# Eight of the 48 modulation bundles leave TensorE's delta-rule chain and are weighed and added on VectorE beside the feed-forward steps

## What is computed

```python
mod = silu_c @ ada_w[i] + ada_b[i]        # [1024] @ [1024, 6 * 1024], for layers i = 0, 1
```

```python
def first_block(x, ...):
    for l in range(DEPTH):                                        # DEPTH = 1
        h = rmsnorm(x, ln1[l])
        proj = h @ w_in[l]
        y_a = gated_deltanet(qkv_a, z_a, b_a, a_a, ...)           # chunked, a triangular solve inside
        y_b = dilated_attention(...)
        x = x + jnp.concatenate([y_a, y_b], axis=-1) @ w_out[l]
        h = rmsnorm(x, ln2[l])
        gate = causal_dwconv(h @ w_gate[l], ffn_conv[l])
        x = x + (jax.nn.silu(gate) * (h @ w_up[l])) @ w_down[l]
    return rmsnorm(x, ln_f)
```

## Time and profile before

| | |
|---|---|
| median of 3 runs | 1216.68 us (1215.64 to 1217.39) |
| the profiled execution's own time | 1214.66 us |
| its span in the profile | 1212.9 us |
| TensorE busy | 1107.1 us, 91% |
| VectorE busy | 593.5 us, 49% |
| ScalarE busy | 431.6 us, 36% |
| GpSimd busy | 94.3 us, 8% |
| read from HBM, written | 351.89 MB, 7.36 MB |

### The profile page before, as it was taken

The page is one execution under the profiler, slowest core; times in us unless marked ns, Lnnn a source line. Parts: engine busy times, 40 slices in busy tenths (PEclk is TensorE's granted clock), DMA queues, the critical chain, the costliest instruction groups (busy, mean ns, idle before and its releaser), DMA issues.

```text
span 1212.9 us, 17412 instructions
## 1 busy us (share of the span) xinstructions
PE 1107.1 (91%) x6792; PEld 741.0 (61%) x6792; DVE 593.5 (49%) x1175; ACT 431.6 (36%) x737; POOL 94.3 (8%) x189
## 2 busy tenths in 40 slices
PE   6998798889999999988999999887999999999986
PEld 6876454779999978855744343324887854343422
DVE  3588543566666656747522322226765532323223
ACT  6445322364444555536411120104545441011200
POOL 0201232320000000013000000002000000000000
PEclk9999999989999999998999999999999999999999
DMA  9956799797777745693679999997676479999996
GB/s 297 263 190 210 273 328 336 203 368 238 212 232 226 227 131 173 209 359 146 265 290 409 409 409 409 409 409 262 224 275 233 142 282 411 409 408 410 409 409 240
DMA packets 164175, 356.15 MB, mean 294 GB/s; under 512 B 10617, under 2 KB 79481, under 8 KB 163969
## 3 DMA queue, kind: packets, MB, share of 16 engines
q1 hardware_dynamic: 147056, 295.81, 67.7%
q0 software_dynamic: 17024, 59.26, 13.9%
q10 hardware_dynamic: 16, 0.02, 0.0%
HBM read 351.89 MB, written 7.36 MB: 296 GB/s over the span
## 4 chain that ended last, share of the span: by engine, by line
PE 67%; DMA 16%; DVE 10%; ACT 4%; issue 2%; POOL 0%; SPq 0%; DVEq 0%; ACTq 0%; POOLq 0%
PE bank L573 35%; PE bank L1134 12%; PE bank L1144 8%; DMA ering<-in_ada_w 4%; DMA ering<-in_moe_w_up 3%; DMA work<-in_moe_w_up 3%; DMA a_raw<-in_moe_w_up 3%; PE bank L1103 3%; DVE wlo L563 2%; PE bank L518 2%; DMA work<-in_ada_w 1%; ACT whi L557 1%; PE bank L741 1%; DMA wraw<-in_w_up 1%; PE bank L1845 1%
## 5 line engine op out<-in xcount | busy, mean ns | idle before, releaser
L563 DVE TENSOR_TENSOR wlo<-wraw,whi 128x1024 fp32r<-128x1024 f32 x150 | 179.3, 1220 | 62.5 <-ACT whi L557 60.3
L557 ACT ACTIVATE whi<-wraw 128x1024 fp32r<-128x1024 f32 x150 | 153.9, 1053 | 55.6 <-PE bank L573 47.1
L573 PE MATMUL bank<-a_hi,whi 128*128 128x256 f32 x512 | 146.7, 287 | 1.5 <-DVE a_lo L771 1.4
L573 PE MATMUL bank<-a_lo,whi 128*128 128x256 f32 x512 | 145.2, 284 | 0.0
L573 PE MATMUL bank<-a_hi,wlo 128*128 128x256 f32 x512 | 145.1, 283 | 0.0
L1134 PE MATMUL bank<-ering,work 128*64 128x512 f32 x576 | 129.6, 595 | 9.4 <-DMA ering<-in_moe_w_up 5.0
L1334 DVE TENSOR_TENSOR work<-work,bank 128x512 f32<-128x512 f32 x16 | 11.0, 687 | 203.7 <-PE bank L1134 203.7
L573 PE MATMUL bank<-whi,a_hi 128*128 128x512 f32 x256 | 102.7, 401 | 4.8 <-DVE a_lo L771 3.0
L1242 ACT ACTIVATE o_hi<-work 128x512 fp32r<-128x512 f32 x32 | 20.2, 630 | 236.7 <-DVE work L1302 236.3
L573 PEld LDWEIGHTS bank<-a_hi,whi 128*128 128x128 f32 x512 | 98.5, 192 | 8.1 <-issue 6.1
L573 PE MATMUL bank<-whi,a_lo 128*128 128x512 f32 x256 | 100.5, 392 | 0.0
(11 more groups left out here) (328 smaller groups left out, 1861.8 us busy)
## 6 DMA issues: line engine op xcount, KB each, us to landing
ering<-in_moe_w_up SPq DMA_DIRECT2D x36, 1024.0 KB, 18.2
ering<-in_moe_w_down SPq DMA_DIRECT2D x36, 1024.0 KB, 18.1
ering<-in_moe_w_gate SPq DMA_DIRECT2D x36, 1024.0 KB, 17.2
ering<-in_ada_w POOLq DMA_DIRECT2D x52, 512.0 KB, 5.7
wraw<-in_w_in SPq DMA_DIRECT2D x28, 512.0 KB, 7.3
work<-in_ada_w POOLq DMA_DIRECT2D x28, 512.0 KB, 8.1
wraw<-in_a_w_qkv SPq DMA_DIRECT2D x24, 512.0 KB, 4.8
work<-in_moe_w_down SPq DMA_DIRECT2D x12, 1024.0 KB, 18.7
```

The costliest lines, as they stand in the source:

```text
L557: nc.scalar.activation(w_hi(c), wraw[:, c % RING, :], ACT.Copy).then_inc(w_hi_done, 1)
L563: nc.vector.tensor_tensor(w_lo(u[0]), wraw[:, u[0] % RING, :], w_hi(u[0]).bitcast(F32), ALU.subtract).then_inc(w_lo_done, 1)
L573: mm = nc.tensor.matmul(out_ap, l, r, start=first and n == 0, stop=last and n == len(terms) - 1)
```

## The change

Bundles 24 to 31 (`ADA_ADDED`) are no longer issued on TensorE. The chain's remaining calls of `ada` are renumbered so that only bundles 8 to 23 stand in it: four ahead of the levels in place of eight, ten in levels 1 to 5 as before, two behind them in place of six. The eight bundles are loaded into three other places of SBUF (11, 12 and 13 of the experts' ring): three of them at the start of the feed-forward layer, the other five during it, one each time that `mul_f` shows a place free. After step 3 + 2j + h VectorE weighs half h of bundle j with one column of silu(c) and adds it to bundle 24's place (`add_bundle`), 16 instructions of 128x1024 elements. VectorE's hardware loop over steps 3 to 20 is written out for that. Behind TensorE's last step four products with a tile of ones sum the weighed rows over the partitions into bank 3, ahead of bundles 35 and 36. Bundles 38 to 40 are loaded behind the last added one. `grow_add(1)` moves from the end of the chain to the first modulated layer, behind `shift_dve`, and the wait on it from the output projection to the second group of qkv columns. `acol_copy(0)` moves from ahead of the levels to level 3, `acol_copy(1)` from level 5 to behind the last copy of the chain.

```diff
-ADA_BANK = [7, 7, 7, 7, 2, 7]
+ADA_BANK = [7, 7, 7, 3, 2, 7]
...
-ADA_BLOCK = 32
+ADA_BLOCK = 24
+
+
+ADA_ADDED = range(24, 32)
+ADA_STEP = 3
...
             if ada_turn(n) > 1:
-                pool.wait_ge(ada_used, max(m for m in range(n) if ada_ring(m) == ada_ring(n)) + 1)
+                m = max(m for m in range(n) if ada_ring(m) == ada_ring(n))
+                if m == ADA_ADDED[0]:
+                    pool.wait_ge(ada_used, ADA_SUM)
+                elif m in ADA_ADDED:
+
+                    pool.wait_ge(mul_f, ADA_STEP + 2 * (m - ADA_ADDED[0]) + 3)
+                else:
+                    pool.wait_ge(ada_used, ada_count(m))
...
-            for n in range(ADA_NORM, ADA_FFN + 1):
-                if ADA_PLACE[n] == 11:
-                    pool.wait_ge(w_used, U_FFN)
+            pool.wait_ge(w_used, U_FFN)
+            for n in (*ADA_ADDED[0:3], *range(ADA_NORM, ADA_NORM + 3)):
                 load_ada(pool, n)
...
+            added = 3
+            for s_ in range(1, FF_STEPS):
+                pool.wait_ge(mul_f, s_)
...
+                if added < len(ADA_ADDED) and s_ == ADA_STEP + 2 * (added - 2) + 3:
+                    load_ada(pool, ADA_ADDED[added])
+                    added += 1
+            for n in range(ADA_NORM + 3, ADA_FFN + 1):
+                load_ada(pool, n)
...
-                ada(10 + c)
+                ada(9 + c)
...
-            ada(12)
+            ada(10)
...
-            ada(14)
+            ada(11)
...
-            ada(16)
+            ada(12)
...
-                ada(15 + 2 * n)
+                ada(11 + 2 * n)
...
-                ada(16 + 2 * n)
+                ada(12 + 2 * n)
...
-            ada(27)
+            ada(23)
...
-            ada(28)
+            ada(24)
...
-            ada(29)
...
-            ada(30)
...
-            ada(31)
...
-            ada(32)
...
             step_pe(pe, FF_STEPS - 1, None, 0)
+            pe.wait_ge(mul_f, ADA_STEP + 2 * len(ADA_ADDED) + 1)
+            for q in range(4):
+                mm = nc.tensor.matmul(psum[ADA_BANK[3]][32 * q:32 * q + 32, :], con[:, C_ONES:C_ONES + 32],
+                                      ada_part(ADA_ADDED[0], q // 2)[:, (q % 2) * HALF:(q % 2 + 1) * HALF], start=True,
+                                      stop=True)
+            mm.then_inc(ada_used, 1)
             ada(ADA_LASTS)
...
             router_weights(psum[3], 0)
-            n = (FF_STEPS - 4) // 2
-            with dve.Fori(0, n) as i:
-                hidden_dve(dve, 3, i, 6, lambda j: split_lo(dve, (nxt[0] + j, i, 6)))
-                hidden_dve(dve, 4, i, 6, lambda j: split_lo(dve, (nxt[0] + 3 + j, i, 6)))
-            nxt[0] += 6 * n
-            for s_ in range(3 + 2 * n, FF_STEPS):
+            def add_bundle(j, h):
+
+                n = ADA_ADDED[j]
+                if h == 0:
+                    dve.wait_ge(ada_in[ada_ring(n)], 32 * ada_turn(n))
+                acc, c = ada_part(ADA_ADDED[0], h), silc[:, j, 0:1]
+                if j == 0:
+                    link(nc.vector.tensor_scalar(acc, acc, c, None, ALU.mult))
+                else:
+                    link(nc.vector.scalar_tensor_tensor(out=acc, in0=ada_part(n, h), scalar=c, in1=acc, op0=ALU.mult,
+                                                        op1=ALU.add))
+
+            for s_ in range(3, FF_STEPS):
                 ffn_step(s_)
+                if 0 <= s_ - ADA_STEP < 2 * len(ADA_ADDED):
+                    add_bundle((s_ - ADA_STEP) // 2, (s_ - ADA_STEP) % 2)
```

49 lines of the change are left out of this document (27 added, 22 removed).

## The result

| | before | with the change |
|---|---|---|
| median | 1217.39 us (9 runs, 1215.64 to 1223.72) | 1209.87 us (9 runs, 1203.58 to 1214.06) |
| ratio, with its 95% interval | | 0.9934 (0.9914 to 0.9955) |
| the profiled execution's own time | 1214.66 us | 1207.93 us |
| its span | 1212.9 us | 1206.1 us |
| TensorE busy | 1107.1 us | 1105.2 us |

The change makes the kernel 7.5 us faster (by the interval, 5.5 to 10.5 us), inside the range of the prediction (1201.5 to 1212.0), with 4.1 us more time than its number, 1205.8. Of these, 0.7 us lie in the kernel before, whose median over nine runs is 1217.39 where the prediction had 1216.68; the gain is 7.5 us where 10.9 were forecast.

What follows compares the result with a forecast made beforehand. The delta rule's chain was taken to be partly led by bundles and their loads in TensorE's fixed order. -8.2 - 3.7 + 1.0 = -10.9 us gave 1203.8 profiled, 1205.8 as median (2.0 above); range 1201.5 to 1212.0.

Steps and rivals of the forecast that it cites:

- Ahead of the levels: Up to the first level: without four bundles VectorE becomes the bound and the first level starts at 149.6, saving 8.2 us.
- the 8 us among its signs: Ahead of the levels: the first level was to come 8 us after L2412's end instead of 18.
- The rival that something else held the chain: Whole chain: the bundles' time is merely relabelled as waiting, so no change, 1216.7 us; chance 0.04.
- Behind the levels: First to last set of `heads`: without bundles the sets follow only data, 8.5 us instead of 12.2, saving 3.7 us.
- The clock among the sets: Sets of `heads`: TensorE was taken to run at the full clock; a granted clock under 1 would show the prediction wrong.
- The second rival: Sets of `heads`: TensorE falls to the lower clock, six sets and the transposes 6 us longer, 1211.8 us; chance 0.11.
- The levels: Levels between the transposes and `heads`: they keep two bundles each and cost the same, 7.7 us for the first.
- Rival 3: Levels: loads of bundles 12 and 13 land up to 1 us late and still lead, 2 us lost, 1207.8; chance 0.08.
- The feed-forward layer: Feed-forward steps: the 16 VectorE adds cost nothing, covered by 1.2 us idle and 2.9 us slack per step; DMA share 0.85.
- Rival 4: Feed-forward layer: VectorE waits in its order for a late bundle, holding the next step; 1226 us if all five late; chance 0.05.
- The end of the layer: Behind TensorE's last feed-forward step: four more products on the path add 1.0 us.
- The tail: Bundle 35 to the end of the span: the distance was to stay at 772.5 us.

Runs made afterwards that it cites:

- the kernel with eight bundles there: The change's sixteen chain bundles placed eight ahead of the levels, two in each of levels 1 to 4, none from level 5 on: 1215.56 us, 0.9985 of the kernel before.
- The four resident products: The change plus four sets of bundle-shaped products on data already in SBUF, results unused, behind sets 1, 3, 5 and 6 of `heads`: 1204.39 us in one run.
- the weights held back: The change with SP's loads of the feed-forward weights held until bundle 23 is used: 1210.01 us in one run.
- The later bundles: The change with one bundle in level 5, 21 and 22 in the last level, 23 ahead of the last set of `heads`: 1203.69 us, 0.9903 of the kernel before.
- the runs with three and four adds: The change with each of VectorE's 14 adds of bundles 25 to 31 issued three or four times: feed-forward steps of 9.40 and 10.71 us in place of 8.5.

## Why the prediction was right, and where it was off

**Ahead of the levels: right.** Forecast -8.2 us, measured -8.3, with the first level at 150.01 (149.6 foreseen), and 18.9 to 19.0 us in all profiles of this code. VectorE was the bound, as the sum had it: the first level came 9.9 us behind the end of the operation that the prediction calls L2412. Its sum gives 10.0; the 8 us among its signs don't fit that sum and are a slip. That TensorE's order, led by loads, was what held it, is shown by the kernel with eight bundles there: 28.0 us, with the waits for loads back. The rival that something else held the chain is out.

**Behind the levels: right, with some luck.** Forecast -3.7, measured -3.6, the gaps among the sets those that were counted. In three other profiles of this code it was 0.6 to 0.9 us less. The four resident products show that the loads were the larger part of it.

**The clock among the sets: right in one profile, not in others.** It was 1.00 in the change's first profile (8.6 us), but 0.92, 0.93 and 0.89 in three others with the same code up to there (9.2 to 9.5 us), and 0.70 with eight bundles ahead (11.4 us). The prediction named a clock under 1 there as a sign that it is wrong. The second rival thus comes true in part and in a smaller size, 0.6 to 2.8 us where it said 6; and in the three profiles the clock had fallen behind a wait for bundle 23's load, not for want of fillers among the sets. The Trainium skill, "TensorE: Matmul & The Clock Gate" (Part 1, on oscillation), describes kernels whose clock goes up and down because matmuls stand between waits for DMA; that is the case at 182.95 us, and in the kernel with eight bundles ahead (0.70 over 141 to 157 us). The rule would have been worth more at the levels than at the sets.

**The levels: the step that failed.** "The levels keep two bundles each and cost the same", a term of nothing in the sum. Measured, from the first level to the first set: 44.5 us against 42.1, so 2.4 us, and 42.5 to 44.0 in four other profiles of this code, on average 1.5 us more. One part is the first level, 8.4 us in all five profiles where 7.7 were taken over from before: behind a gap of 2.96 us the low clock now lasts into the bundle, which took 1.94 us. Filler in that gap brought the level to 6.9. The other part is from the second level to the first set. Before, in the change's first profile, and with the resident products, where the clock was 1.00:

```profile
165.49:199.88 34.39, 30.30 (x519) 18.41 (x515) 14.76 (x30) 10.40 (x18) 10.46 (x20) 1.00 0.97 341
```

```profile
158.41:194.49 36.08, 32.62 (x518) 19.95 (x514) 14.87 (x30) 10.49 (x18) 8.37 (x16) 0.91 0.88 303
```

```profile
157.49:191.65 34.16, 30.16 (x518) 18.31 (x514) 14.78 (x30) 10.49 (x18) 8.38 (x16) 1.00 0.93 323
```

TensorE stood for 4.1 us of this stretch before, for 3.5 in the change's first profile and for 4.0 to 4.5 in the four others, so the waits hardly grew. What grew is its busy time, 30.3 to 32.6 us for the same products, at a clock of 0.91. Where the clock stayed at 1.00 the stretch took 34.2 us and cost the same, as forecast. So what the prediction missed is the clock behind the waits that stay. With the wait of 2.79 us and the slow products behind it level 5 took 10.6 us in place of 6.7 (and the last level, which had waited before, 4.9 in place of 7.1). When the clock falls is left open: it fell behind waits for loads of 1.84 to 2.79 us in four of the five profiles of this code, and did not behind one of 1.92 us in the one profile of the kernel before. Rival 3 had loads that still lead, and about the price (2 us lost), but at bundles 12 and 13 and as waits; they led at 20 to 23, and the price was mostly the clock's.

Why the loads of 20 to 23 are late is in part argued. The levels' own ten bundles ask for about 305 GB/s, where full stretches moved 351 (with the weights held back) to 386, and weights come in beside them. The transfers of 8.60 and 8.27 us in the chain before, from 183.10 and 193.65 us, could have warned of it. The later bundles show that place decides it: with the same 16, 3 to 5 us less from first level to first set, and no wait for a load.

**The feed-forward layer: right in its result, wrong in its limit.** The steps take the same 8.5 us with VectorE at 123.9 of 161.4 us and the DMA share at 0.86 (0.85 foreseen). The 2.9 us of slack was named as cover for each step; the runs with three and four adds fit the other reading, that only the 3.0 us which VectorE has to spare in a step count. With 1.28 us of adds neither limit is reached, so no number of the forecast came out otherwise. Rival 4, a late bundle that holds VectorE, did not occur: no wait of VectorE in these steps is for a load.

**The end of the layer: right.** +1.0 forecast; 430.96 - 430.07 = 0.89 us.

**The tail.** The forecast held it constant. The profile after has 2.6 us more behind bundle 35 than the one before; but the profiles of this code range from 771.9 to 776.4, on either side of the 772.5 of before. The difference stands in the last stretch, from 700 us behind bundle 35 to the end, first before and then in the change:

```profile
1140.37:1212.90 72.53, 55.15 (x244) 18.88 (x238) 19.89 (x33) 4.98 (x8) 0.00 (x0) 0.99 0.85 338
```

```profile
1130.96:1206.10 75.14, 57.37 (x246) 20.15 (x242) 20.18 (x33) 4.97 (x8) 0.00 (x0) 0.93 0.83 329
```

The granted clock goes with it, and the resident products, with the change's code there, have 71.88 us at 0.99. It is not shown that the change has a part in it; but six of the seven profiles lie above 774, and with one profile of the kernel before, of a run 2.7 us under its median, it isn't excluded either. So of the 3.4 us between 10.9 forecast and 7.5 measured, 1.5 on average, and 2.4 in the profile, is the failed step. The rest can't be told from what runs of one kernel differ by: the change's two sets of runs give gains of 7.5 and 11.8 us.

## What to carry to other kernels

Work that is moved off a chain pays by where it stood, not by how much it was: four bundles less ahead of the levels were worth 8 us, while the same sixteen with eight ahead of them brought nothing that can be told in the time as a whole. When a chain gets shorter, ask of each load behind it whether its distance still covers its transfer at the share that the stretch will have, and count the clock behind a long wait as well as the wait; place such filler last in the waits that nothing else can fill. Slack of a consumer in a repeated step can be spent once, while the time that an engine has to spare in each step can be spent in each. And a distance that is forecast to stay the same deserves several profiles, before and after: here five of the change differ by 2 us in one stage.

## What was not expected of the hardware

The time of a run follows the mean granted clock of the core, closely enough to tell runs of one kernel apart. Over 15 runs of the change (1202.22 to 1214.06 us, clock 0.971 to 0.985) the correlation is -0.91, and 0.001 of clock goes with 0.8 us. Both kernels read off at a clock of 0.978, the change is at 1208.5 us and the kernel before (33 runs, its correlation -0.72) at 1217.3, so 8.8 us apart, a little more than the medians of the first set say. The clock is not independent of the kernel, since waits lower it, so this is a reading and not a correction.

ScalarE's table load (1.28 us) and the two activations behind it were mostly hidden as long as a bundle stood beside them; with the bundle elsewhere TensorE waited 1.84 us for what followed them, and in one profile the 64 products behind the wait ran at the lower clock too, 3.50 us in place of 2.08.
